# Attention heads in pairs: where a head's projections, value rows and turned key weights stand in the order of work

## What is computed

```
q      = (c_q @ w_q_b)   -> 8 heads of 128 + 64 (rotary)      # c_q: 384 wide
w_uk   = w_kv_b[..., :128]      # per head, 256 x 128: keys
w_uv   = w_kv_b[..., 128:]      # per head, 256 x 128: values
s      = (q . k) * scale, causal;  p = softmax(s);  o = p @ v
q_lat  = einsum('bthn,chn->bthc', q_nope, w_uk)    # for the sample tokens
```

## Time and profile before

| what | value |
|---|---|
| time, three runs | 3492.95, 3501.75 and 3504.45 us, median 3501.75 |
| profiled execution | 3500.34 us, of which the span of the engines is 3498.5 |
| TensorE busy | 3303.9 us, 94% of the span |
| VectorE, ScalarE, GpSimd busy | 52%, 38%, 35% |
| the four iterations | about 139 to 626 us of the span |
| mean granted clock of TensorE | 0.966 of full |

### The profile page before, as it was taken

The page is one execution under the profiler, slowest core; times in us unless marked ns, Lnnn a source line. Parts: engine busy times, 40 slices in busy tenths (PEclk is TensorE's granted clock), DMA queues, the critical chain, the costliest instruction groups (busy, mean ns, idle before and its releaser), DMA issues.

```text
span 3498.5 us, 72361 instructions
## 1 busy us (share of the span) xinstructions
PE 3303.9 (94%) x26364; PEld 2948.1 (84%) x26364; DVE 1826.5 (52%) x3142; ACT 1345.1 (38%) x2810; POOL 1214.3 (35%) x847
## 2 busy tenths in 40 slices
PE   9999999999999999999999888888889999999998
PEld 6676766678899999997899877777778899999998
DVE  3454545213644377866203567666732464447785
ACT  2232323431454444322214455556521154453332
POOL 0000000010466677731223222223213066677771
PEclk9999999999999999999999989989978999999999
DMA  3121210630344554432223101100052045454442
GB/s 106 52 76 57 58 58 17 198 117 1 95 157 157 165 166 136 136 107 76 74 74 108 68 13 44 32 26 26 18 147 85 13 130 158 158 180 136 136 145 84
DMA packets 303577, 331.50 MB, mean 95 GB/s; under 512 B 54350, under 2 KB 285825, under 8 KB 303138
## 3 DMA queue, kind: packets, MB, share of 16 engines
q1 hardware_dynamic: 297346, 309.17, 27.9%
q0 software_dynamic: 6048, 19.73, 1.8%
HBM read 232.57 MB, written 116.69 MB: 100 GB/s over the span
## 4 chain that ended last, share of the span: by engine, by line
PE 60%; PEld 6%; DVE 5%; issue 4%; POOL 3%; ACT 2%; DMA 1%; SPq 0%; ACTq 0%; DVEq 0%; PEldq 0%; POOLq 0%
PE bank L615 58%; PEld bank L615 6%; PE bank L623 2%; POOL wloA L1953 1%; POOL arena L1953 1%; POOL wloS L1953 1%; DVE arena L3363 1%; DVE hT L3429 1%; SPq L1586 0%; ACT hT L2627 0%; DVE arena L3380 0%; DVE arena L2877 0%; DMA arena<-arena 0%; ACT arena L2177 0%; DVE arena L3067 0%
## 5 line engine op out<-in xcount | busy, mean ns | idle before, releaser
L615 PE MATMUL bank<-arena 128*128 128x268 f32 (+20 forms) x8302 | 1162.8, 333 | 77.9 <-ACT arena L2177 25.2
L615 PEld LDWEIGHTS bank<-arena 128*128 128x128 f32 (+7 forms) x8302 | 878.9, 178 | 339.7 <-issue 113.8
L1953 POOL TENSOR_TENSOR arena<-arena 128x512 f32<-128x512 f32 x120 | 165.7, 1381 | 1213.4 <-DMA arena<-in_ffn_w_up 766.9
L2177 ACT COPY arena<-bank 128x512 f32<-128x512 f32 (+14 forms) x557 | 252.6, 487 | 816.4 <-PE bank L615 590.9
L2357 ACT ACTIVATE whiS<-arena 128x512 fp32r<-128x512 f32 x180 | 113.0, 628 | 407.1 <-POOL arena L1953 393.9
L1953 POOL TENSOR_TENSOR wloA<-arena,whiA 128x512 fp32r<-128x512 f32 x180 | 262.4, 1471 | 0.4 <-ACT whiA L2354 0.4
L1953 POOL TENSOR_TENSOR wloS<-arena,whiS 128x512 fp32r<-128x512 f32 x180 | 238.9, 1341 | 49.1 <-ACT whiS L2357 49.1
L3229 DVE TENSOR_TENSOR hT<-hT,bank 128x536 f32<-128x536 f32 x280 | 197.4, 706 | 82.4 <-PE bank L615 82.0
L615 PE MATMUL bank<-hiT,whiS 128*128 128x268 f32 x768 | 199.9, 289 | 7.3 <-DVE loT L3071 3.7
L623 PE MATMUL bank<-table,arena 128*128 128x128 f32 (+5 forms) x1354 | 171.6, 268 | 26.1 <-DMA arena<-in_x_prompt 7.2
L3076 DVE TENSOR_TENSOR arena<-std,bank 128x268 f32<-128x268 f32 x192 | 80.4, 432 | 215.7 <-PE bank L615 209.3
(11 more groups left out here) (297 smaller groups left out, 8093.9 us busy)
## 6 DMA issues: line engine op xcount, KB each, us to landing
u_scratch<-arena SPq DMA_DIRECT2D x480, 134.0 KB, 1.8
arena<-in_ffn_w_up SPq DMA_DIRECT2D x64, 512.0 KB, 4.2
arena<-u_scratch SPq DMA_DIRECT2D x56, 536.0 KB, 5.1
arena<-in_ffn_w_down SPq DMA_DIRECT2D x112, 256.0 KB, 3.9
arena<-u_scratch SPq DMA_DIRECT2D x56, 402.0 KB, 6.0
arena<-past_scratch SPq DMA_DIRECT2D x32, 640.0 KB, 8.0
past_scratch<-in_cache_kv_latent SPq DMA_DIRECT2D x128, 128.0 KB, 2.4
past_scratch<-in_cache_k_rope SPq DMA_DIRECT2D x128, 32.0 KB, 2.1
```

The lines of the kernel that those rows point to most:

```text
L615: return pe.matmul(out, lhsT, rhs, start=first, stop=last, skip_group_check=group)
L1953: return pool.tensor_tensor(out, a, b, op)
L2177: lane.do(act.copy(dst, b if view is None else view(b)), ring.drained)
```

## The change

The work is the same, instruction for instruction; its order differs on TensorE, and on ScalarE and VectorE to match.

- The pieces of `hh` 0 are projected at the start as before. The pieces of `hh` 1 are projected in steps 10, 11 and 12 of `hh` 0, one in each, ahead of that step's `values`, whose wait then leaves out the last fill of `ra` (`since` 1).
- The key weights are turned first, directly ahead of the first scores. There the waits are for all of `ra` but the last fill, and for all of `rv` (`hh` 0) or all but the last (`hh` 1).
- The value rows go behind the scores of steps 0, 1 and 2, and the sample's queries behind those of step 2. With them `wkv_used` is signalled later.

```
+                for p in range(3):
+                    project(0, p)
                 for hh in range(2):
-                    for at, w in PIECES:
-                        product(ra, lambda j: wq[:, j, hh * 192:hh * 192 + NOPE], lambda j: cq[:, j, at:at + w], 3, w=w)
-                        product(rv, lambda j: wkv[:, j, hh * 256:hh * 256 + NOPE], lambda j: ckv[:, j, at:at + w], 2, w=w)
-                    for t0, n in [(0, 4), (4, 4), (8, 2)]:
+                    b = ra.bank()
+                    for k in range(2):
+                        ins = turn(b[:, k * P:(k + 1) * P], wkv[:, k, hh * 256:hh * 256 + NOPE], P)
+                    ra.done(ins)
+
+                    def value_rows(t0, n):
                         b = ra.bank()
...
-                    ra.wait_drained()
-
-                    rv.wait_drained()
-                    b = ra.bank()
...
+                    def sample_queries():
+
+                        ra.wait_drained(3)
+                        b = ra.bank()
+                        for k in range(2):
+                            ins = mm(b[:, k * ND:(k + 1) * ND], wukT[:, k * P:(k + 1) * P], qn[hh][:, NP:T], True, True)
+                        ra.done(ins)
+                        if hh == 1:
+                            wkv_t.add(pe.drain())
+
+                    ra.wait_drained(1)
+                    rv.wait_drained(hh)
...
-                    def values(n_):
+                    def values(n_, since=0):
                         q = Q_ORDER[n_]
-                        ra.wait_drained()
+                        ra.wait_drained(since)
...
                     for n in range(NQ + 3):
+                        ahead = hh == 0 and n >= NQ
                         if n < NQ:
                             scores(Q_ORDER[n])
+                        if ahead:
+                            project(1, n - NQ)
+                        if n < 3:
+                            value_rows(4 * n, min(4, NQ - 4 * n))
+                        if n == 2:
+                            sample_queries()
                         if n >= 3:
-                            values(n - 3)
+                            values(n - 3, 1 if ahead else 0)
                         if 2 <= n <= NQ + 1:
                             turn_probs(n - 2)
```

On ScalarE:

```
                     for n, q in enumerate(Q_ORDER):
+                        if n < 3:
+                            rows = min(4, NQ - 4 * n)
+                            take(vtok[0:QT, 4 * n * VH:(4 * n + rows) * VH], QT, rows * VH)
+                        if n == 2:
+                            take_sample_queries()
                         if n >= 2:
                             turn(n - 2)
...
+                    if hh == 0:
+                        take_queries_of(1, 0)
                     turn(NQ - 2)
+                    if hh == 0:
+                        take_queries_of(1, 1)
                     turn(NQ - 1)
+                    if hh == 0:
+                        take_queries_of(1, 2)
```

More of the change, by code:

```diff
@@ L759, in _, with project @@
                     product(rv, lambda j: rot, lambda j: qraw[:, at:at + w], 1, w=w)
-                for hh in range(2):
-                    for at, w in PIECES:
-                        product(ra, lambda j: wq[:, j, hh * 192:hh * 192 + NOPE], lambda j: cq[:, j, at:at + w], 3, w=w)
-                        product(rv, lambda j: wkv[:, j, hh * 256:hh * 256 + NOPE], lambda j: ckv[:, j, at:at + w], 2, w=w)
-                    for t0, n in [(0, 4), (4, 4), (8, 2)]:
+                def project(hh, p):
+                    at, w = PIECES[p]
+                    product(ra, lambda j: wq[:, j, hh * 192:hh * 192 + NOPE], lambda j: cq[:, j, at:at + w], 3, w=w)
+                    product(rv, lambda j: wkv[:, j, hh * 256:hh * 256 + NOPE], lambda j: ckv[:, j, at:at + w], 2, w=w)
+                for p in range(3):
+                    project(0, p)
+                for hh in range(2):
+                    b = ra.bank()
[3 more added lines that the diff above has]
+                    def value_rows(t0, n):
                         b = ra.bank()
@@ L770, in _ @@
                         ra.done(ins)
-                    b = ra.bank()
-                    for k in range(2):
-                        ins = turn(b[:, k * P:(k + 1) * P], wkv[:, k, hh * 256:hh * 256 + NOPE], P)
-                    ra.done(ins)
-                    ra.wait_drained()
-                    rv.wait_drained()
[L778 to L783, removed]
+                    def sample_queries():
[8 more added lines that the diff above has]
+                    rv.wait_drained(hh)
                     def scores(q):
@@ L2255, in _, with take_queries_of, take_sample_queries @@
                 exp_t.enter(i, 2 * NQ)
+                def take_queries_of(hh, p):
+                    at, w = PIECES[p]
+                    take(qn[hh][:, at:at + w], P, w)
+                for p in range(3):
+                    take_queries_of(0, p)
                 for hh in range(2):
[L2257 to L2260, removed]
                     take(wukT, P, 2 * P)
[L2262 to L2266, removed]
+                    def take_sample_queries():
+                        b = ring.bank()
+                        for k in range(2):
+                            ins = act.copy(qlat[:, k, :, bass.ds((i * 2 + hh) * DS, DS)],
+                                           b[:, k * ND:(k + 1) * ND].rearrange("p (b q) -> p b q", q=DS))
+                        lane.do(ins, ring.drained)
                     def turn(n_):
@@ L2944, in _, with take_keys_of @@
                                             qpe[half, NP:T].rearrange("p (b q) -> p b q", q=DS)))
+                def take_keys_of(hh, p):
+                    at, w = PIECES[p]
+                    take(kn[hh][:, at:at + w], P, w)
+                for p in range(3):
+                    take_keys_of(0, p)
                 for hh in range(2):
-                    for at, w in PIECES:
-                        take(kn[hh][:, at:at + w], P, w)
                     def maxima(n_):
@@ L2984, in _ @@
                             scaled(n - 1)
+                        if hh == 0 and n >= NQ:
+                            take_keys_of(1, n - NQ)
                         if n >= 3:
```

## The result

The changed kernel took 3475.0 us, the median of five runs (3472.7 to 3477.8), beside 3501.5 for the kernel before (3493.0 to 3504.5). The ratio is 0.9933, with a 95% interval of 0.992 to 0.9947. The profiled execution took 3475.72 us with a span of 3473.9, against 3500.34 and 3498.5: 24.6 us less.

A forecast was written before the change was run, and what follows sets the result against it. TensorE, busy for 94% of the span, was taken as the bound, with gains only where it waits or loses clock. 3500.3 - 23.1 (waits) - 4.5 (clock) = 3472.7, so 3473 us was predicted, range 3463 to 3489.

The forecast's parts named there:

- The sum over waits: TensorE in the heads: waits removed less new waits, 1.70 + 2.07 + 2.61 - 0.6 = 5.8 us an iteration, 23.1 for four.
- the four new ones at the first scores: First heads' first scores: four new waits for the keys' copy, some 0.4 us idle each, priced at 0.6 us an iteration.
- 0.16: At each TensorE wait: overlap between successive rows is lost too, so a wait costs its idle time and 0.16 us.
- Cover for the probabilities: Before the first turns: 5.0 us of cover against 1.7 needed, so both waits for probabilities go, 2.07 us an iteration.
- 3.3 us of room left: Before the first turns: what remains of 5.0 us of cover after the chain's 1.1 + 0.6 = 1.7 us.
- The rival that had the waits replaced in part: Start of each head: one longer wait takes up to half the gain, about -12 us, 3488 us; chance 0.10.
- SyncE: Page copies and weight loads: `wkv_used` comes about 7 us later, some 35 us of room remain, nothing on the path.
- The clock: End of the first iteration's first head: the fall to 1.2 GHz was expected to go, another 4.5 us.
- the rival in which the clock's loss stays: Heads' ends: waits go but one end falls as before, in another iteration, 3500.3 - 23.1 = 3477 us; chance 0.25.
- The last step of my sum: Whole time: from 3472.7 us, with the profiled execution 1.4 us below the median of 3501.75, to a predicted 3473.

The follow-up runs named there:

- the kernel before with turns first: Kernel before, with only the turns of the next tile's probabilities put ahead of the values in steps 10 to 12 of both heads: 3474.9 us, ratio 0.993.
- the run before it: Changed kernel, with the next tile's turns put ahead of the values in steps 10 to 12 of the second head: 3459.3 us, ratio 0.988.
- The rotary kernel: Changed kernel, with the first head's first query piece projected between the rotary products and the wait for their copies: median 3466.6 us, ratio 0.9901.

## Why the prediction was right, and where it was not

**The sum over waits** gave 5.8 us an iteration; steady iterations became 6.23 us shorter (119.74 to 113.51). The places were right: the waits that were to go are gone, and the four new ones at the first scores are 0.42 us idle each, as expected. What was missing is a second small price. The first two rows behind a wait of the kernel before last 0.46 us together, where two at the pace of their kind would last 0.38 (0.27 for one and a distance of 0.11):

```profile
321.34 0.46 PE L615 MATMUL bank<-arena 104*128 104x104 f32 x2 [0.67 <-ACT arena L2177]
```

So the row behind a wait is some 0.08 late again. Seven waits fewer and one more make 6 x 0.07 = 0.4, which is nearly all of the difference. This price was set after the first result, and the experiments tested it. With idle + 0.16 + 0.07 the runs came out at 116.88, 117.04, 117.12, 111.49, 112.60, 109.92 and 109.37 where 116.9, 117.0, 117.0, 111.7, 112.6, 109.9 and 109.2 were expected. (The 115.7 for the kernel before with turns first, which came out at 115.70, was twice the gain measured in the run before it, and no test of the price.) That this restart costs the same at every wait was not measured apart.

**Cover for the probabilities.** I had 3.3 us of room left; the trace shows 3.6. The copy of value rows did stand ahead of the exponential, which started at 281.65, right behind it, and no wait came of it. The rival that had the waits replaced in part is out: only the fraction at the last keys was.

**SyncE.** The order was right and the size was not: I put the signal 7 us later, and the weights were issued 1.8 us later into the iteration. The 7 us are the scores of three tiles (28 rows, 7.26 us). I left out that six of the waits that go stand ahead of the signal, and the new one too: by the price above 0.92 x 2 + 1.16 + 2.82 - 0.65 = 5.2 us, which leaves 2.1. It was off the path both times.

**The clock** is the step that failed. I wrote that the fall at the end of the first iteration's first head would go, and that this would be another 4.5 us. It went from there, but the second head's end of the same iteration fell instead, for 116.79 - 113.51 = 3.3 us, and the copies began 1.2 us later (151.33 and 150.10), for the same 18 rows at the start of the loop took longer at a lower clock (0.79 and 0.63 of full over 138 to 146 us), before and after:

```profile
137.91 7.36 PE L615 MATMUL bank<-arena 128*128 128x384 f32 x18 [1.43 <-POOLq L595]
137.84 8.65 PE L615 MATMUL bank<-arena 128*128 128x384 f32 x18 [1.42 <-POOLq L595]
```

In place of 4.5 the clock gave 1.2 at the fall and took 1.2 at the start, so nothing. That is the rival in which the clock's loss stays, which I gave 0.25. The waits alone are 4 x 6.23 = 24.9 us, and the heads gave 24.8. So the time came out close in part by luck: the missing 4.5 us and the 1.8 that the waits gave more (24.9 against 23.1) have opposite signs, and the median of 3475.0 lies as near to the rival's 3477 as to my 3473. The last step of my sum has a slip too: 3472.7 with the 1.4 us of the median added is 3474, not 3473.

**Which ends fall.** I counted over all profiles, leaving out the last end of each, behind which the stage changes. Ends of heads with the three waits of 0.7 us in them: 33, of which 8 ran at half clock. Ends without: 51, none. The last ends, up to where TensorE stops for the pages, go the same way: 5 of 7 with the waits, none of 5 without. The rotary kernel had none of three in one execution and three of three in the other, so the ends of one execution are not independent of each other, and twelve executions are few. All falls seen at ends stood at ends with the waits; that none is possible without them is not shown. The waits don't decide it either: in the 4 us ahead of each of the eight falls TensorE was busy for 2.55 to 2.75 us, and so it was at ends that kept the full clock, while without the waits it is busy for longer. One end of each kind, a fall (changed kernel), none with the waits (kernel before), none without (turns first):

```profile
249.12:253.12 4.00, 2.65 (x24) 2.24 (x22) 0.77 (x3) 1.40 (x5) 0.00 (x0) 1.00 0.24 74
322.50:326.50 4.00, 2.55 (x24) 2.13 (x22) 0.66 (x3) 1.39 (x4) 0.00 (x0) 1.00 0.00 0
372.50:376.50 4.00, 3.36 (x13) 1.93 (x11) 1.61 (x4) 0.00 (x0) 0.00 (x0) 1.00 0.16 44
```

What decides is open, since it differs between executions of one program. The rule of the Trainium skill (TensorE: Matmul & The Clock Gate, "Why this matters for your kernels") that it takes long idle gaps does not hold here: the longest idle time ahead of these falls was 0.73 us. Its advice, to keep TensorE busy, agrees with the counts.

## What to carry to other kernels

Price a wait of a pipelined engine by the distance between starts and not by the idle time shown: here 0.69 us idle was 0.85 to 0.92. Before work is brought from elsewhere as cover, look whether the order of two neighbours does it: in the kernel before, turns before values in both heads, a few lines, gave 4.0 us an iteration, and moving a head's projections alone gave 2.9. Compare versions by the length of a steady iteration in the trace where whole times depend on the clock: one run each put two kernels here 5.5 us apart, and the medians of four runs put them 12.8 apart the other way round.

## What the runs showed of the hardware that I had not expected

The granted clock of TensorE went to 0.50 (1.2 GHz) behind 4 us in which it was busy for 2.55 to 2.75 us and at no time idle for as long as 1 us, and the same program did so in one execution and not in the next: 3.2 to 4.5 us each time. Whether a loop without such ends makes whole times steadier is open. Without them they spread over 3447.0 to 3452.7, 3448.5 to 3455.2 and 3473.8 to 3481.0 in four runs each and 3455.0 to 3460.2 in five; the changed kernel, which has them, over 3472.7 to 3477.8 in five, and the kernel before over 3490.7 to 3507.5 in the 14 runs of one session.
